# The gap between the weights' rings and the operand tiles: 64 bytes in place of 960

## The reference, cut to what matters

```
for i in range(DEPTH):                      # first block, two layers
    u = rmsnorm(h) @ w_in[i]                # 2048 x 5632: conv value, glu, gate, q, k, v, gate
    ya = conformer_conv(...) * silu(a_z)    # depthwise conv of 31 taps, layer norm
    yb = window_attention(...) * silu(b_z)
    h = h + concat([ya, yb]) @ w_out[i]     # 2048 x 2048
    h = h + rmsnorm(p[i] @ w_pe[i]) * sigmoid(h @ w_pg[i])
# second block: a layer of forgetting attention (2048 x 8224 in, 2048 x 2048 out)
# and a layer of sliding window attention (2048 x 4608 in, 2048 x 2048 out)
```

## Time and profile before

| | |
|---|---|
| median of 3 runs | 1818.62 us |
| the profiled execution | 1819.21 us |
| its span, first to last instruction | 1817.4 us |
| TensorE, products (PE) busy | 98% |
| TensorE, weight loads (PEld) busy | 93% |
| VectorE busy | 72% |
| ScalarE busy | 50% |
| mean DMA rate | 179 GB/s |

### The profile page before, as it was taken

The page is one execution under the profiler, slowest core; times in us unless marked ns, Lnnn a source line. Parts: engine busy times, 40 slices in busy tenths (PEclk is TensorE's granted clock), DMA queues, the critical chain, the costliest instruction groups (busy, mean ns, idle before and its releaser), DMA issues.

```text
span 1817.4 us, 35698 instructions
## 1 busy us (share of the span) xinstructions
PE 1780.4 (98%) x14365; PEld 1683.5 (93%) x14365; DVE 1312.5 (72%) x2088; ACT 902.5 (50%) x1326; POOL 41.9 (2%) x48
## 2 busy tenths in 40 slices
PE   8999999999999999999999999999999999999997
PEld 7998999999999999999999898998989999999876
DVE  7898889886779987988777755555565656666654
ACT  5333565545543455446564353545455443565553
POOL 0000000000000000000000110100000000000000
PEclk9999999999999999999999999999999999999999
DMA  7576645565656664555565656565655665545463
GB/s 234 176 209 183 186 140 172 165 198 197 193 185 210 187 191 139 157 192 180 182 196 181 198 180 203 173 196 183 185 159 157 187 185 178 154 138 157 157 191 131
DMA packets 199826, 325.54 MB, mean 179 GB/s; under 512 B 14783, under 2 KB 66191, under 8 KB 199565
## 3 DMA queue, kind: packets, MB, share of 16 engines
q1 hardware_dynamic: 197085, 320.85, 57.0%
q10 hardware_dynamic: 2608, 2.84, 0.5%
HBM read 320.42 MB, written 2.69 MB: 178 GB/s over the span
## 4 chain that ended last, share of the span: by engine, by line
PE 78%; DVE 15%; ACT 3%; issue 1%; DMA 1%; POOL 0%; ACTq 0%; SPq 0%; DVEq 0%; POOLq 0%
PE g L491 60%; PE g L502 9%; DVE w_lo L900 6%; DVE cacc L1146 6%; PE att L587 2%; PE att L610 2%; PE att L630 2%; ACT w_hi L1521 2%; ACT u L1530 1%; DMA stage<-in_fox_w_in_dram 0%; DVE u L1025 0%; PE att L780 0%; ACT L1530 0%; DVE q L921 0%; DMA cacc<-in_norm_g_dram 0%
## 5 line engine op out<-in xcount | busy, mean ns | idle before, releaser
L900 DVE TENSOR_TENSOR w_lo<-stage,w_hi 128x1024 fp32r<-128x1024 f32 x577 | 708.0, 1234 | 425.1 <-ACT w_hi L1521 424.6
L1521 ACT CAST w_hi<-stage 128x1024 fp32r<-128x1024 f32 x577 | 598.5, 1049 | 639.1 <-PE g L491 438.5
L491 PE MATMUL g<-a_hi,w_hi 128*128 128x256 f32 x2496 | 708.4, 284 | 5.9 <-DVE w_lo L900 4.9
L491 PE MATMUL g<-a_hi,w_lo 128*128 128x256 f32 x2496 | 696.6, 279 | 0.0
L491 PE MATMUL g<-a_lo,w_hi 128*128 128x256 f32 x2496 | 696.5, 279 | 0.0
L491 PEld LDWEIGHTS g<-a_hi,w_hi 128*128 128x128 f32 x2496 | 472.3, 189 | 20.1 <-issue 15.8
L491 PEld LDWEIGHTS g<-a_lo,w_hi 128*128 128x128 f32 x2496 | 471.9, 189 | 0.0
L491 PEld LDWEIGHTS g<-a_hi,w_lo 128*128 128x128 f32 x2496 | 470.4, 188 | 1.5 <-issue 1.2
L491 PE MATMUL g<-b_hi,w_hi 128*128 128x256 f32 x1440 | 404.9, 281 | 2.9 <-DVE w_lo L900 1.9
L491 PE MATMUL g<-b_hi,w_lo 128*128 128x256 f32 x1440 | 401.5, 279 | 0.0
L491 PE MATMUL g<-b_lo,w_hi 128*128 128x256 f32 x1440 | 401.5, 279 | 0.0
(11 more groups left out here) (231 smaller groups left out, 1385.0 us busy)
## 6 DMA issues: line engine op xcount, KB each, us to landing
stage<-in_fox_w_in_dram SPq DMA_DIRECT2D x128, 512.0 KB, 3.9
stage<-in_w_in_dram SPq DMA_DIRECT2D x112, 512.0 KB, 3.8
stage<-in_swa_w_in_dram SPq DMA_DIRECT2D x72, 512.0 KB, 3.8
stage<-in_w_in_dram SPq DMA_DIRECT2D x128, 256.0 KB, 3.1
stage<-in_w_out_dram SPq DMA_DIRECT2D x64, 512.0 KB, 4.2
stage<-in_w_pg_dram SPq DMA_DIRECT2D x64, 512.0 KB, 4.0
stage<-in_fox_w_out_dram SPq DMA_DIRECT2D x32, 512.0 KB, 4.5
stage<-in_swa_w_out_dram SPq DMA_DIRECT2D x32, 512.0 KB, 4.5
```

The lines of the kernel that those rows point to most:

```text
L491: mm = pe.matmul(acc[:, j * S:(j + 1) * S], w[:, slot, c0 + j * P:c0 + (j + 1) * P], xx[:, k, :], start=st and m == 0 and j % 2 == 0, stop ...
L900: dve.tensor_tensor(w_lo[:, slot, :], stage[:, slot, :], w_hi[:, slot, :].bitcast(F32), ALU.subtract).then_inc(*t.inc("w_split"))
L1521: act.copy(w_hi[:, slot, :], stage[:, slot, :]).then_inc(*t.inc("w_rounded"))
```

## The change

The constant that sizes the unused tile `apart` goes from 240 to 16 floats:

```
-APART = 240
+APART = 16
```

## The result

The changed kernel took 1837.61 us (median of 4 runs, 1833.12 to 1839.06) against 1818.57 us before: a ratio of 1.0097 with a 95% interval of 1.0076 to 1.0117. It is slower, by 19 us where 9 were forecast. Its profiled execution took 1836.81 us, its span is 1835.0 us, and the granted clock 0.999 as before.

What follows compares the result with a forecast made beforehand. The prediction took TensorE to bound the kernel (PE busy 98%, 78% of the chain), its identical products having two pitches. Form T's +9 us, all else 0, on 1818.6 gave about 1828 us, range 1801 to 1845.

Steps and rivals of the forecast that it cites:

- the likeliest case: Whole kernel: half of form T's floor stretches turn slow, about 1828 us, own range 1822 to 1833, chance 0.29.
- the prediction's own signs: Long L491 pieces: some stretches from about 392 and 863 at 117.8 ns, others at 113.4, mean about 117 over 25.
- (a): Form T gemm products, about 11,800: half of the floor stretches go to the slow level, +9 us in all.
- plus 64 is bad throughout: Rival: form T at 117.85 ns or a little more everywhere, 1839 us, up to 1850 at 120 ns; chance 0.21.
- Plus 64 knows the same two levels: Form T with operands 64 above the weights: both pitches, about 113.3 and 118 ns, occur there too.
- the role swap: KV chunk: form N, moving operand 64 above its stationary one, stands in for form T; six products at 113.3 ns.
- The pe row: Products of `pe_hi` and `pe_lo`, 128 below the weights: 11 pitches at 118.2 ns each, read as never settled, about slow.
- (b): Form N, some 800 products: between 1.8 us back and 3 us lost, taken as 0.
- (c): The 192 products of `pe_hi` and `pe_lo`, going to distance 0: -1 to +0.4 us, taken as 0.
- (d): Attention, norms, convolution and transfers, which move with the operands by 896 bytes: 0 with 1 us either way.
- The loss beside the convolution: Form T pieces beside VectorE's taps and splits: a slower TensorE costs 1 or 2 us, at most 6.
- The distance doesn't decide: Rival: levels come from the phase of the weight load, not addresses; nothing changes, 1818.6 us; chance 0.17.

Runs made afterwards that it cites:

- experiment 2: Kernel before with no gap between weights and operands, so operands at distance 0: 1852.07 us, ratio 1.0154.
- experiment 1: Kernel before with the gap cut from 960 to 448 bytes, operands again 64 below the weights modulo 512: 1825.33 us, ratio 1.0003.
- experiment 3: Changed kernel's 64-byte gap plus 896 unused bytes behind `b_lo`; against the kernel before only `a_hi` to `b_lo` move: 1836.36 us, ratio 1.0067.
- experiment 4: Kernel before with 128 unused bytes between `a_lo` and `b_hi`, putting `b_hi` and `b_lo` 64 above the weights: 1828.84 us, ratio 1.0026.

## Why the prediction was right, and where its size failed

The time of 1837.6 us lies inside the range of 1801 to 1845, but outside the 1822 to 1833 that the likeliest case had for itself. The reading that identical products have two pitches, and that the change alters which of them a stretch has, was right. The direction was right partly by luck: it was reached through the KV piece, in which form N was to stand in for form T, and that stand-in is refuted below. By the prediction's own signs the forecast case did not come: both stretches from 392 and 868 are slow, not one of them, and the long pieces average 118.0 ns (24 of them, 6138 products in 724.2 us) and not 117.

**The step that was mis-sized is (a)**, "a loss of half of the floor stretches", +9 us with the convolution's stretch. All the long ones lost the floor: the 1068 (4.7 us), the 876 (3.9), the 396 from 1071.89 (1.7) and the half of the 396 from 1271.64 that had it (0.9), together 11.3 of the 11.9 that were priced for "all at 117.85". The rest of the 17.6 us is short pieces and form N, less the 1.9 that the two stretches of 216 gave back. The rival "plus 64 is bad throughout", priced at 1839, with a chance of 0.21, is nearly the true case (1837.6). It isn't true throughout: the two stretches of 216 went to the floor. Its branch of 120 ns belongs to distance 0 (experiment 2). "Plus 64 knows the same two levels" stands for those 216 and not for a stretch of 396 or more.

The argument that halved the loss was the role swap: form N of a KV chunk "is form T with the roles swapped", and its five floor pitches after 116.61 were taken to show the floor at 64 above. Swapped roles would give form N, after the change, the moving operand 64 below the stationary one and so the floor; it went up instead, from 229.6 to 234.0. At distance 0 form T is at its slowest (120.0) and form N at its fastest (227.6). The pe row was the better witness: it is form T at another distance, with means of 118.2 at 128 below, 120.0 at 0 and 113.3 at 64 below. That it "settles on neither" level can't be read from it, as its starts are given to 10 ns; form T 128 above took 118.7, a level of its own. The prediction also took a level to change only beside other products or at a change of form; the 396 from 1271.64 change inside, at a short pause (experiment 1). And of the 25 longest pieces 24, not 22, are of L491 (6276 products, 728.1 us, 116.0 each), which moves its sums by 1 us.

**(b), form N, was taken at 0 and cost about 3 us**: the 282 took 1.25 us more (64.76 to 66.00), and at that rate, 4.4 ns, the 756 products with 512 columns would make 3.3, an estimate that is a little high, since some pieces of 36 were at 233.3 before. Its upper end, "all of them 3 us", was the right one.

**(c)** was right in place and size: 118.2 to 120.0, inside the stretch that VectorE bounds. **(d)**, 0 with 1 us either way, held: experiment 3 puts all of the rest back and about 1 us goes with it.

**The loss beside the convolution** (1 or 2 us taken, 6 at most) was 0. The changed kernel entered the first layer's convolution 0.46 us behind (52.11 against 51.65) and left it 0.44 behind (165.47 against 165.03); in the second layer it was 4.80 behind before it (525.16 against 520.36) and 4.79 after it (641.02 against 636.23). The 156 and the 372 products there were at the slow level already. The 162 from 564.61 were at the floor and lost it, but the chain after the change runs there over VectorE's taps and splits, so it didn't come out.

**"The distance doesn't decide"** is refuted by experiment 4 within one stream: the sequence of instructions is the same and only addresses moved. The rule of the Trainium skill that the prediction weighed, that TensorE's ports never wait on anyone (page "SBUF — State Buffer", section "SBUF: two separate sides"), gives no effect at all; the runs don't agree with that outcome, as the kernels with the operands at 0 and at 64 below differ by 1.5 to 2%, though none of them shows a port waiting. What did not stand is the bound of 0.2% for what can be told from no change. It came from three runs within 3 us of each other; 23 runs on another chip spread over 12 us, which fits long stretches that change level between executions.

What stays open: why a stream that may stand at the floor stands at one level in one execution and at the other in the next, and why only some stretches do; why 64 above held the floor for 216 products and for none of the long stretches; whether the distance or the operand's own address counts; what it is in the two reads that has a period of 256 bytes; and why form N answers to the placement in another way. None of the runs measures these by itself.

## What to carry to other kernels

When long runs of identical matmuls show more than one pitch, divide length by count for each piece of the chain and compare levels before looking at any wait: 4.5 ns a product was 1% of this kernel. The place of the operands, modulo 256 bytes in this case and with the weights held still, decides whether a long stretch can reach the fast level. An unused tile of some bytes is a cheap knob, and all products of a stream should have the good distance, not most of them. Take the price of a placement from the same instruction at another address, as pe's products gave it, and not from another form; and since which level a stretch gets may be a matter of chance, time such a knob with many runs.

## What the runs showed of the hardware that was not expected

- A float32r product with 256 moving columns takes 113.35 ns at its floor and 117.3 to 120.0 otherwise, by the place of its operands; with 32 stationary columns it took 113.5 to 114.2 (5.45 to 5.48 us for 48) at gaps of 0, 64 and 960 bytes, at which the full one took 120.0, 117.8 and 113.35. That speaks for the weight load as the other party, which is argued and not shown. The narrow product isn't wholly free of the effect: at gaps of 416, 464 and 480 bytes the 48 took 5.61 us, 116.9 each, and at 128 bytes 5.55.
- The address period is 256 bytes: gaps of 0 and 256 gave 128.15 us for the same 1068 products, and 192, 448 and 960 the same 64.75 or 64.76 us for the 282 of form N.
- The good place is narrow: 64 and 80 below are good; 48 and 96 below cost 1.6 and 1.3%.
- The level follows the tile within a few products at a handover (experiment 4), and can change at a pause of two pitches of 0.23 and 0.22 us with the tiles unchanged (experiment 1).
- At the good place the same kernel's executions spread over 12 us on one chip; four runs at 48 below (1843.65 to 1845.69) and four at 256 (1852.15 to 1853.52) over about 2, the four after the change (1833.12 to 1839.06) over 6.
